# Seven products in a third unit of each second strip pair, with ScalarE copying the banks out and VectorE adding them later

## The reference: what is computed

```python
h2 = rms_norm(x, g_mlp[layer])
x = x + jnp.square(jax.nn.relu(h2 @ w_mlp_in[layer])) @ w_mlp_out[layer]
return rms_norm(x, g_final)
```

## Time and profile before

| | |
|---|---|
| median of three runs | 1630.11 us |
| the profiled execution, its own time | 1630.46 us |
| its span, first to last instruction | 1628.6 us |
| TensorE (PE) | busy 1616.6 us, 99% |
| VectorE (DVE) | busy 1215.4 us, 75% |
| ScalarE (ACT) | busy 898.4 us, 55% |
| granted TensorE clock, mean | 0.999 |

### The profile page before, as it was taken

The page is one execution under the profiler, slowest core; times in us unless marked ns, Lnnn a source line. Parts: engine busy times, 40 slices in busy tenths (PEclk is TensorE's granted clock), DMA queues, the critical chain, the costliest instruction groups (busy, mean ns, idle before and its releaser), DMA issues.

```text
span 1628.6 us, 20399 instructions
## 1 busy us (share of the span) xinstructions
PE 1616.6 (99%) x7974; PEld 1361.0 (84%) x7974; DVE 1215.4 (75%) x1470; ACT 898.4 (55%) x1248; POOL 79.0 (5%) x67
## 2 busy tenths in 40 slices
PE   9999999999999999999999999999999999999998
PEld 7888888888888888888888888888888888888886
DVE  7887778877666677766565567996699768986793
ACT  6666656766565445554444555654565455555562
POOL 3000000000000134000000000000000000000000
PEclk9999999999999999999999999999999999999999
DMA  7666665666556664445565775457635863576461
GB/s 270 193 207 201 187 188 188 206 195 205 174 186 185 190 186 154 143 143 179 182 234 193 259 235 190 157 206 235 190 125 202 273 190 130 207 262 189 144 233 52
DMA packets 134192, 312.19 MB, mean 192 GB/s; under 512 B 9744, under 2 KB 10448, under 8 KB 133968
## 3 DMA queue, kind: packets, MB, share of 16 engines
q1 hardware_dynamic: 129376, 302.21, 56.8%
q10 hardware_dynamic: 4720, 8.68, 2.1%
HBM read 308.68 MB, written 2.16 MB: 191 GB/s over the span
## 4 chain that ended last, share of the span: by engine, by line
PE 87%; DVE 9%; issue 2%; DMA 1%; ACT 1%; POOL 0%; POOLq 0%; ACTq 0%; DVEq 0%
PE G L1599 18%; PE G L1600 17%; PE G L1601 17%; PE S L1608 7%; PE G L1608 7%; PE G L1612 4%; PE S L1612 4%; PE S L1599 3%; PE S L1601 3%; PE S L1600 3%; DVE wlo L951 3%; DVE wlo_late L951 2%; PE S L1620 1%; DMA raw<-in_w_in 1%; DVE raw L954 1%
## 5 line engine op out<-in xcount | busy, mean ns | idle before, releaser
L602 ACT ACTIVATE whi<-raw 128x1024 fp32r<-128x1024 f32 x377 | 398.4, 1060 | 395.7 <-PE G L1601 317.0
L951 DVE TENSOR_TENSOR wlo<-raw,whi 128x1024 fp32r<-128x1024 f32 x377 | 461.0, 1236 | 133.6 <-ACT whi L602 132.8
L1599 PE MATMUL G<-whi,a_both 128*128 128x512 f32 x960 | 376.8, 393 | 2.2 <-DVE wlo L951 2.2
L1601 PE MATMUL G<-whi,a_both 128*128 128x512 f32 x960 | 373.8, 389 | 0.0
L1600 PE MATMUL G<-wlo,a_both 128*128 128x512 f32 x960 | 373.8, 389 | 0.0
L1599 PEld LDWEIGHTS G<-whi,a_both 128*128 128x128 f32 x960 | 180.3, 188 | 39.9 <-issue 2.8
L1601 PEld LDWEIGHTS G<-whi,a_both 128*128 128x128 f32 x960 | 180.2, 188 | 37.8
L1600 PEld LDWEIGHTS G<-wlo,a_both 128*128 128x128 f32 x960 | 180.4, 188 | 35.7
L1599 PE MATMUL G<-whi,b_hi 128*128 128x512 f32 x328 | 128.5, 392 | 0.3
L1600 PE MATMUL G<-wlo,b_hi 128*128 128x512 f32 x328 | 128.0, 390 | 0.0
L1601 PE MATMUL G<-whi,b_lo 128*128 128x512 f32 x328 | 127.7, 389 | 0.0
(11 more groups left out here) (283 smaller groups left out, 2591.7 us busy)
## 6 DMA issues: line engine op xcount, KB each, us to landing
raw<-in_w_in SPq DMA_DIRECT2D x208, 512.0 KB, 4.1
raw<-in_w_mlp_in SPq DMA_DIRECT2D x64, 512.0 KB, 4.3
gates<-in_w_mlp_in SPq DMA_DIRECT2D x64, 512.0 KB, 3.7
raw<-in_w_mlp_out SPq DMA_DIRECT2D x64, 512.0 KB, 4.9
gates<-in_w_mlp_out SPq DMA_DIRECT2D x64, 512.0 KB, 4.9
raw<-in_w_ssm_up SPq DMA_DIRECT2D x32, 512.0 KB, 3.6
raw<-in_w_attn_up SPq DMA_DIRECT2D x32, 512.0 KB, 4.0
raw<-in_w_out SPq DMA_DIRECT2D x32, 512.0 KB, 4.6
```

The costliest lines, as they stand in the source:

```text
L602: act.activation(high(m), piece(n), ACT.Copy).then_inc(hi_made, 1)
L951: dve.tensor_tensor(low(m), piece(n), high(m).bitcast(F32), ALU.subtract).then_inc(lo_made, 1)
L1599: pe.matmul(out_ap, hi[:, k, cols], w_hi, start=start, stop=False)
L1601: return pe.matmul(out_ap, lo[:, k, cols], w_hi, start=False, stop=stop)
```

## The change

Units 0, 1 and 2 of every second pair are crossed, in place of 1 and 2. The second pair's order becomes: pieces 0 and 1 of unit 3, unit 0, unit 1, piece 2 of unit 3, unit 2, piece 3 of unit 3. Unit 0 gets sums of its hidden part as well. `sums` and `mix` are replaced in groups 0 to 2: ACT copies four banks out in two instructions of 128x1024, `carry_out` the first pair's plain banks and `mix_out` a pair's mixed banks, at a place in its stream *ahead* of the splits of that step; DVE adds the copies in the next group's first two `mlp_in` windows (`sums`, `mixed`). To make room, the MLP's ring of raw slots has seven places instead of eight. The load of `g_last` moves from the first `mlp_in` window to the last pair. Group 3 keeps the old way of mixing.

The core of the diff:

```diff
     def pair(g, q, before):
         window(4 * g + 21 + q, 0, "mlp_pair", (g, q, 0), before)
-        window(4 * g + 21 + q, 1, "mlp_pair", (g, q, 1), [("mix", (g, q))])
+        window(4 * g + 21 + q, 1, "mlp_pair", (g, q, 1), [("mix_out", (g, q))])
...
-            window(4 * g + 19, 0, "mlp_in", (g, 0), [("sums", (g - 1, 1))])
+            window(4 * g + 19, 0, "mlp_in", (g, 0), [("sums", g - 1), ("mixed", (g - 1, 0))])
...
-            pair(g, 1, [("sums", (g, 0))])
+            pair(g, 1, [("carry_out", g)])
...
-CROSSED = (1, 2)
-MIX_AT = max(4 * CROSSED[-1] - 4, 0)
+LATE_RAW = LATE_RING - 1
+CROSSED = {0: (1, 2), 1: (0, 1, 2)}
+SUMMED = (0, 1, 2)
+PAIR_ORDER = {
+    0: tuple((unit, part) for unit in range(4) for part in range(4)),
+    1: ((3, 0), (3, 1), (0, 0), (0, 1), (0, 2), (0, 3), (1, 0), (1, 1), (1, 2), (1, 3), (3, 2), (2, 0), (2, 1), (2, 2),
+        (2, 3), (3, 3)),
+}
+MIX_OUT = {0: 4, 1: 7}
...
 def piece_slot(n):
-    return n % RING if n < N_MLP else (n - N_MLP) % LATE_RING
+    return n % RING if n < N_MLP else (n - N_MLP) % LATE_RAW
...
+        def carry_out(p, g, pr, pp):
+            if p == 0:
+                act.wait_ge(used, done(pr, pp))
+                act.wait_ge(hid_lo, 4 * g + 4)
+                for h in range(2):
+                    act.activation(tmp_both[:, 2 * h * N:2 * (h + 1) * N], wide(G, h), ACT.Copy).then_inc(c_out, 1)
+
+        def mix_out(p, idx, pr, pp):
             g, q = idx
...
+            if p != MIX_OUT[q]:
+                return
+            act.wait_ge(used, pair_done(g, q, CROSSED[q][-1]))
...
+            for h in range(2):
+                act.activation(wide(m_acc[q], h), wide(G if q else S, h), ACT.Copy).then_inc(m_out, 1)
...
             for p in range(PIECES):
+                for name, at in sides:
+                    if name in before_splits:
+                        before_splits[name](p, at, *previous(r, par))
                 for m in due(piece_number(r, par, p), LEAD_HI):
                     split(m)
...
+        def sums(p, g, pr, pp):
+            if p < 2:
+                dve.wait_ge(used, done(pr, pp))
...
+            if p == 2:
+                dve.wait_ge(c_out, 2 * g + 2)
+                own = x_sb[:, 0:2, :, :].rearrange("p a b n -> p (a b n)")
+                dve.tensor_tensor(own, own, tmp_both, ALU.add).then_inc(c_added, 1)
...
+                if (unit, part) == PAIR_ORDER[q][0]:
+                    if q:
+                        pe.wait_ge(m_out, 2 * turn)
...
+                if (unit, part) == (CROSSED[q][0], 0):
+                    pe.wait_ge(s_lo_made, len(SUMMED) * (g + 1))
+                    if q:
+                        pe.wait_ge(c_out, 2 * (g + 1))
...
-                    pe.wait_ge(mix_v, 8 * idx[0])
+                    pe.wait_ge(m_out, 4 * idx[0])
```

More of the change, by code:

```diff
@@ L552, in window @@
                         sp.dma_start(x_sb[:, c, :, :], x_k[:, :, c * N:(c + 1) * N]).then_inc(s_x[c], 16)
-                if kind == "mlp_in" and first(idx[0]) and (idx[1], p) == (0, 0):
-                    sp.wait_ge(used, done(16, 1))
+                if kind == "mlp_pair" and (idx, p) == ((3, 0, 0), 0):
+                    sp.wait_ge(x_mixed, 6)
                     sp.dma_start(g_last[:, :], g_final.rearrange("(a n) -> a n", a=1).to_broadcast([P, D])
@@ L884, in hidden @@
                 act.wait_ge(used, done(pr, pp))
-                if g or j > CROSSED[0]:
-                    act.wait_ge(s_lo_made, len(CROSSED) * g + sum(u < j for u in CROSSED))
+                if g or j > SUMMED[0]:
+                    act.wait_ge(s_lo_made, len(SUMMED) * g + sum(u < j for u in SUMMED))
+                if g and j == 0:
+                    act.wait_ge(c_added, g)
                 act.activation(hidden_t, hidden_banks(j)[:, :, T:2 * T], ACT.Copy).then_inc(hid_t, 1)
@@ L1412, in mix, with mix_out @@
+        def mix_out(p, idx, pr, pp):
+            g, q = idx
+            if g == 3 and p == MIX_OUT[q]:
+                dve.wait_ge(mix_a, 1)
                 for i, (out_ap, of, bank) in enumerate(((mt[:, 1, 1, :], mt[:, 0, 0, :], 1), (mt[:, 0, 1, :], mt[:, 1, 1, :], 2),
@@ L1455, in _ @@
         table = {f.__name__: f for f in (rates, decays, conv, scan, tables, zgate, rope, attend, gated_a, merged,
-                                         residual, hidden, mix, sums, finish)}
+                                         residual, hidden, sums, mixed, mix_out, finish)}
         def window(r, par, kind, idx, sides):
@@ L1818, in seven @@
                     "b21": sums_bank(q, 0, 0), "b22": sums_bank(q, 1, 0), "t4": sums_bank(q, 0, 1)}
-            first_one, last_one = (start, stop) if block in ("b11", "t2", "t3", "t1") else (False, False)
+            if block in ("b11", "t2", "t3", "t1"):
+                first_one, last_one = start, stop
+            else:
+                first_one, last_one = False, (block, q, unit) == ("b22", 1, 2)
             if block in left:
@@ L1824, in seven @@
                 i, tb = ("t1", "t2", "t3", "b22").index(block), 0
-                hi, lo = (s[:, CROSSED.index(unit), i, :, :] for s in (s_hi, s_lo))
+                hi, lo = s_hi[unit][:, i, :, :], s_lo[unit][:, i, :, :]
             for kk in range(2):
@@ L1854, in pair_window @@
                         pe.wait_ge(lo_made, BLOCK[n] + i + 1)
-                        seven(PAIR_BLOCKS[i], q, unit, BLOCK[n] + i, unit == CROSSED[0], unit == CROSSED[-1]
+                        seven(PAIR_BLOCKS[i], q, unit, BLOCK[n] + i, unit == CROSSED[q][0], unit == CROSSED[q][-1]
                               ).then_inc(used, 1)
@@ L1864, in pair_window @@
                             last = three_passes(sums_bank(q, half, tb), k, tb, b_hi, b_lo, high(m)[:, cols],
-                                                low(m)[:, cols], k == 0, k == KT - 1)
+                                                low(m)[:, cols], (unit, kk) == (PAIR_ORDER[q][0][0], 0) and kh == 0,
+                                                k == KT - 1 and (q, half, tb) != (1, 1, 0))
                     last.then_inc(used, 1)
```

129 lines of the change are left out of this document (75 added, 54 removed).

## The result

The changed kernel takes **1632.68 us** (median of 22 runs, 1629.58 to 1634.71), the kernel before 1630.05 (22 runs, 1629.65 to 1630.34): a ratio of 1.0016 [1.0009, 1.0022]: 2.6 us slower, which by the bound of 0.2% counts as no change, though the interval's upper end passes it. The forecast was 1631.9 us and "no change". One thing did not fit it from the start: the changed kernel's runs spread over 5 us, those of before over 0.7.

The account below looks back on a forecast made before the run. PE's stream bounds the kernel, busy 1616.6 of 1628.6 us. Fewer matmuls (-4.08), a removed wait (-1.19) and a new stall (+7.0) sum to +1.8 us on 1630.11: 1631.9 us, no change, range 1624.5 to 1635.

Parts of the forecast that it names:

- The gains: PE's second pairs, groups 0 to 2: 18 fewer matmuls, 4.08 us, and no wait for DVE's adds, 1.19; together 5.27 us.
- the stall at the second pair's first crossed block: PE waits there for DVE's adds out of G, 0.40 us in each of groups 0 to 2; removing it gains 1.19 us.
- The crossed units: Second pair: DVE keeps ahead of PE through units 0 to 2, with 1.16 us to spare at unit 2's block 4.
- the rival in which DVE comes late: Second pair: DVE reaches unit 1 late and becomes the bound in unit 2; 2 us late gives 1637.9 us; chance 0.2.
- The new stall: Head of the next mlp_in window, groups 0 to 2: PE waits for mix_out's copies behind M5, 2.34 us each, 7.0 us.
- the bounds: M5's transfer, taken as 4.9 us: 3.5 as when alone gives a 0.94 us stall, 5.5 gives 2.94.
- The sum: Whole kernel: -4.08 - 1.19 + 7.0 = +1.8 us (-2.5 to +3.6 with the transfer's bounds), giving 1631.9 us.
- The cover: The mlp_in windows: 18 us of DVE's adds and sums fit into 28 us of spare time and cost nothing.
- The spacing of matmuls: PE's stream: 0.227 us a matmul from the trace; by the skill's 131 ns the gain would be 2.4 us, time 1633.6.

Follow-up runs that it names:

- two experiments: Changed kernel with second pair's copies of G behind M2, 1624.58 us; changed kernel with unit 0 of second pairs plain again, 1628.78 us.
- The other two profiles: The changed kernel run again twice without any edit, one run each: 1633.85 and 1635.14 us.
- the four versions without a fall: Changed kernel with second pair's copies behind M2, 1624.58; behind M4, 1626.93; unit 0 uncrossed, 1628.78; one wait for each copy, 1627.96 us.
- the best version: Changed kernel with the second pair's two copies of G three high parts earlier on ScalarE, behind M2 instead of M5: 1624.58 us, ratio 0.9964.
- the first profile of the copies behind M6: Changed kernel with the second pair's two copies of G one high part later on ScalarE, behind M6 instead of M5: 1639.83 us, ratio 1.0054.
- the changed kernel's third profile: The changed kernel run once more without any edit, to count stretches at the lower clock: 1635.14 us.
- the second run of the copies behind M6: Changed kernel with the second pair's copies of G behind M6 instead of M5, run once more without further edit: 1641.04 us.

## Why the prediction was right, and where it was short

**The gains.** Right. 18 matmuls fewer, 4.08 us predicted, 4.20 measured between two experiments; the stall at the second pair's first crossed block, 0.40 a time, is gone. Together they gave 1630.05 - 1624.58 = 5.5 us, where the prediction has 5.27.

**The crossed units.** Right to 0.1 us. These rows are the second pair of group 1 in the changed kernel, where x = 0 is PE's start at 1239.65 (the first row); then DVE at unit 1, unit 2 and from unit 2's block 4 on:

```profile
1239.65 0.39 PE L1664 MATMUL G<-whi_late,b_hi 128*128 128x512 f32 x1
```

```profile
1241.00 1.23 DVE L988 TENSOR_TENSOR wlo_late<-gates,whi_late 128x1024 fp32r<-128x1024 f32 x1 [1.31 <-ACT whi_late L619]
...
1255.02 1.22 DVE L988 TENSOR_TENSOR wlo_late<-gates,whi_late 128x1024 fp32r<-128x1024 f32 x1
...
1264.49 2.35 DVE L988 TENSOR_TENSOR wlo<-gates,whi 128x1024 fp32r<-128x1024 f32 x2
1266.77 1.22 DVE L988 TENSOR_TENSOR wlo_late<-raw,whi_late 128x1024 fp32r<-128x1024 f32 x1
```

DVE waits 1.31 us (about 1.2 predicted) and begins unit 1 at x = 1.35 (1.35), unit 2 at 15.37 (15.36), and is done with block 6 at 28.34 (28.31). That wait is why the rival in which DVE comes late did not happen: the reserve was there, and DVE began unit 1 when PE freed the place.

**The new stall.** Right in place, cause and chain. SP, ACT and the last column of SP's issue (us to landing) show it:

```profile
1268.01 0.37 SPq L592 DMA_DIRECT2D raw<-in_w_mlp_in  x1
```

```profile
raw<-in_w_mlp_in SPq DMA_DIRECT2D x1, 512.0 KB, 4.8
```

```profile
1272.82 1.06 ACT L619 ACTIVATE whi<-raw 128x1024 fp32r<-128x1024 f32 x1 [0.52 <-DMA raw<-in_w_mlp_in]
1273.78 1.92 ACT L938 ACTIVATE m_acc<-G 128x1024 f32<-128x1024 f32 x2
```

M5 is issued at x = 28.36 (28.34), takes 4.8 us (4.9, where the bounds were 3.5 and 5.5), ACT begins its high part at 33.17 (33.25) and PE starts M0 at 36.10 instead of 34.00. The stall is 2.10 us and 0.11 on the next matmul; 2.34 predicted. The sum over the three is 5.95 + 0.33 = 6.3 us against **7.0**, so the term was too large for this execution. The other two profiles have 5.94 + 0.33 = 6.3 and 7.07 + 0.33 = 7.4 us: 7.0 lies between them. That the stall comes from the copies' place behind M5 is shown by moving them: none, 0.7, 2.0 and 3.5 us of mean stall behind M2, M4, M5 and M6.

**What was left out.** The sum priced a stall at its own length, and PE's restart at 0.10 us on the second matmul. The lower clock behind a stall has no term in it: some 1.57 us each, two in each of three profiles of the changed kernel. In the profiled execution the two errors are -0.7 us (the stalls) and +3.1 us (two falls), so that it took 1633.84 us. Without falls it would be 1624.58 + 6.28 = 1630.9 us; the median, 1632.68, lies 1.8 above that, which by an estimate from these rows is about one fall per run (1.8 / 1.57), if the stalls of the median run are those of the profiled one. The granted clock of the 22 runs gives a like estimate: 0.9974 on average against 0.9988 in the four versions without a fall, at 0.001 for each fall (3.41 us at half of 1632), so 1.3 falls per run; the two runs at 0.999 took 1629.58 and 1630.56 us, the two at 0.996 1633.74 and 1634.71. "No change" did not hang on luck, as 1630.9 us without a fall is no change either. That the median came within 0.8 us of the forecast is in part luck: in the profiled execution the two errors have opposite signs. The earlier trace rows could not show it: no stretch of the MLP before has a stall of 2 us.

**The cover.** Right. Four `mlp_in` windows of group 1 have DVE busy 74.65 of 89.28 us, 13.6 more than the 61.05 of the earlier trace rows (those are group 2's windows; 18 predicted), and PE has no gap in them. The 18 was too much from the start: four of its adds, 2.7 us, stood in these windows before the change too (`sums` of the second pair).

**The spacing of matmuls.** The prediction took 0.227 us a matmul from the row; the runs hold to it (4.20 / 18 = 0.233). The Trainium skill (TensorE: Matmul & The Clock Gate, section "Back-to-back issue gap") gives about 131 ns for 512 columns in a sustained stream; here the trace and the runs disagree with it, and the measurement decides.

## What to carry to other kernels

A copy that frees PSUM for PE is worth as much as its place in its engine's queue: look which transfer the instruction ahead of it waits for, and put the copy ahead of work that PE wants later, as far as there is time for it: in the best version ACT stands still for 1.66 us in front of the copies, and PE waits for none of the splits behind them. Here three places earlier were worth 8 us, and the same change went from no gain to 5.5 us of it. A stall of PE can cost more than its length: after it, look at the granted clock of the next few us, and where runs spread more than before, count such stretches in more than one profile.

## What was not expected of the hardware

After PE had stood still for 2 to 4 us, its granted clock was 0.50 for 3.41 us (twice 6.83) in eleven of thirteen cases; the two without a fall had stalls of 2.35 and 3.36 us, and the shortest with a fall was 2.07. In the first profile of the copies behind M6 the clock fell 0.1 and 1.1 us before PE started again (1278.53 against 1278.63, 1452.61 against 1453.68), in the changed kernel 0.3 and 1.2 us after. Behind the eight stalls of 0.22 to 1.73 us it did not fall. So the length of a stall alone does not decide; what else does stays open. The load of the DMA does not tell the cases apart: in the changed kernel's third profile it moved 401 GB/s in the 3.4 us behind the stall of 2.35 us (1104.70 to 1108.10, no fall) and 387 behind that of 2.07 (1276.31 to 1279.70, a fall). The matmuls at the lower clock, in the second run of the copies behind M6:

```profile
1281.17 1.05 PE L1676 MATMUL G<-a_both,whi_late 128*128 128x512 f32 x2
1282.03 0.63 PE L1680 MATMUL G<-a_both,wlo_late 128*128 128x256 f32 x2
1282.45 1.05 PE L1676 MATMUL G<-a_both,whi_late 128*128 128x512 f32 x2
```

Four matmuls, two of 512 and two of 256 columns, take 1282.45 - 1281.17 = 1.28 us; at full clock the same four take 0.70 (a block of sixteen 2.79). The Trainium skill (TensorE: Matmul & The Clock Gate, section "Back-to-back issue gap") gives the spacing of isolated matmuls at the lower clock, in ns, as columns divided by 1.2; an estimate by it is 1.28 us for these four, and the trace agrees.
